# One pass of a GLA + S5 + RG-LRU trunk layer: six bands of GLA moved into the LRU stage, with changes of order in S5, merge and tail

## The reference

```
mod  = silu(c) @ w_ada + b_ada                   # shift, scale, gate, twice
proj = (x * (1 + scale1) + shift1) @ w_in        # q, k, v, r, glr, u, lx, ly, gates
LRU  : conv of lx, gates ga/gi (sigmoid), h_t = a_t h_(t-1) + sqrt(1-a_t^2) i_t x_t, both ways, * gelu(ly)
GLA  : log_a = log_sigmoid(glr @ w + b) / 16; chunked S_t = diag(a_t) S_(t-1) + k_t v_t, o_t = q_t S_t,
       both ways, normed, * silu(r)
S5   : h_t = A h_(t-1) + B u_t (complex), y = Re(C h) + d u, both ways; gelu; y * sigmoid(y @ w_glu)
merged = g_gla*(y_gla @ w) + g_s5*(y_s5 @ w) + g_lru*(y_lru @ w)     # g = sigmoid(gates)
x = layer_norm(alpha x + gate1 * (merged @ w_out))
y = layer_norm(alpha x + gate2 * (relu(mlp_in(x))^2 @ w_mlp_out))    # also returned: the final states
```

## Time and profile before

| what | us |
|---|---|
| runs | 3119.44, 3128.88, 3127.63 (median 3127.63) |
| the profiled execution, own time | 3128.83 |
| its span, first to last instruction | 3127.0 |
| TensorE (PE) busy | 2897.6 (93%) |
| VectorE (DVE) busy | 1786.0 (57%) |
| ScalarE (ACT) busy | 1163.8 (37%) |
| GpSimd (POOL) busy | 767.6 (25%) |
| mean granted TensorE clock | 0.963 of full |

### The profile page before, as it was taken

The page is one execution under the profiler, slowest core; times in us unless marked ns, Lnnn a source line. Parts: engine busy times, 40 slices in busy tenths (PEclk is TensorE's granted clock), DMA queues, the critical chain, the costliest instruction groups (busy, mean ns, idle before and its releaser), DMA issues. The chain is left out here.

```text
span 3127.0 us, 41861 instructions
## 1 busy us (share of the span) xinstructions
PE 2897.6 (93%) x17008; PEld 2795.7 (89%) x17008; DVE 1786.0 (57%) x2397; ACT 1163.8 (37%) x1761; POOL 767.6 (25%) x363
## 2 busy tenths in 40 slices
...
PEclk9999988989999699899998999999999999999998
...
GB/s 215 52 64 60 64 19 63 31 26 29 42 32 21 54 98 171 123 118 126 130 98 166 112 191 122 205 132 164 84 34 41 48 41 41 42 47 41 41 44 65
DMA packets 111164, 257.82 MB, mean 82 GB/s; under 512 B 20944, under 2 KB 54736, under 8 KB 110736
## 3 DMA queue, kind: packets, MB, share of 16 engines
...
...
## 5 line engine op out<-in xcount | busy, mean ns | idle before, releaser
L2539 PE MATMUL bank<-yhi,mrg_hi 128*128 128x384 f32 x1560 | 526.3, 337 | 3.3 <-POOL mrg_lo L2482 1.8
L2539 PE MATMUL bank<-ylo,mrg_hi 128*128 128x384 f32 x1560 | 522.9, 335 | 0.0
L2539 PE MATMUL bank<-yhi,mrg_lo 128*128 128x384 f32 x1560 | 522.8, 335 | 0.0
L2482 POOL TENSOR_TENSOR mrg_lo<-mrg_raw,mrg_hi 128x1024 fp32r<-128x1024 f32 x69 | 169.5, 2457 | 678.5 <-ACT mrg_hi L2641 678.5
L2506 PE MATMUL bank<-yhi,mrg_hi 128*128 128x384 f32 x864 | 293.0, 339 | 39.9 <-POOL mrg_lo L167 24.3
L2539 PEld LDWEIGHTS bank<-yhi,mrg_hi 128*128 128x128 f32 x1560 | 293.9, 188 | 6.9 <-POOL mrg_lo L2482 2.6
L2539 PEld LDWEIGHTS bank<-ylo,mrg_hi 128*128 128x128 f32 x1560 | 293.8, 188 | 1.2 <-issue 0.3
L2539 PEld LDWEIGHTS bank<-yhi,mrg_lo 128*128 128x128 f32 x1560 | 293.8, 188 | 0.0
L2506 PE MATMUL bank<-ylo,mrg_hi 128*128 128x384 f32 x864 | 290.8, 337 | 0.0
L2506 PE MATMUL bank<-yhi,mrg_lo 128*128 128x384 f32 x864 | 290.7, 336 | 0.0
L1720 PE MATMUL bank<-hhi,s_hi 128*128 128x384 f32 x768 | 265.1, 345 | 22.5 <-POOL s_lo L180 19.3
...
## 6 DMA issues: line engine op xcount, KB each, us to landing
...
```

Of the source, the lines that this page charges most:

```text
L2482: pool.tensor_tensor(WLO[SLOT[u]], S.raw[u % 2], WHI[SLOT[u]].bitcast(F32), ALU.subtract).then_inc(S.split_done, 1)
L2539: mm = pe.matmul(out, wt[SLOT[u]][:, w], r[:, k, band_cols(b)], start=(k == first and y == 0), stop=(k == last and y == 2))
```

## The change

- The weight buffers belong to `Core` and are shared by all stages. The LRU stage loads four of GLA's units, splits three, and TensorE makes six GLA bands behind the last LRU gate products, into banks 0, 1, 5, 6, 7, 2. ACT's `evac_y(11)` stands behind `roots(11)`. GLA begins with the evacuation of six bands, then band 6.
- S5: the tables' stores move up in SP's queue, between u loads; two lead bands stand behind `transposes(0)`; `powers` is cut in two and moved behind bands 6, 7, 9 and 10; four bands a slot for ten slots (was eleven), two in the last (was one).
- Merge: fills 4 to 8 on ACT and 4 to 7 on DVE are made inside the last GLU round; the load of a later tile is issued by another rule; the second tile of LRU weights is loaded ahead of the `y_out` wait.
- Tail: running sums on POOL, `rstd` of the last band ahead of six of eight `final`, sum of squares in halves, the last two `final` on DVE, y stored in other pieces.

The diff without context (line numbers of the old file; indentation inside a hunk reduced; "..." marks hunks that only pass names):

```diff
@@ L56
+AHEAD = 2
+AHEAD_BANK = (0, 1, 5, 6, 7, 2)
@@ L105
+self.raw, self.hi, self.lo = ([ctx.enter_context(nc.sbuf_tensor(f"w_{part}{s}", [P, UW], dt)) for s in range(2)]
+                              for part, dt in (("raw", F32), ("hi", F32R), ("lo", F32R)))
@@ L126
-def __init__(self, core, ctx, name, raw_width=UW):
-    nc = core.nc
+def __init__(self, core, name):
-    self.memory = ctx.enter_context(nc.sbuf_tensor(f"{name}_raw", [P, 2 * raw_width], F32))
-    self.raw = [self.memory[:, s * raw_width:s * raw_width + UW] for s in range(2)]
-    self.hi = [ctx.enter_context(nc.sbuf_tensor(f"{name}_hi{s}", [P, UW], F32R)) for s in range(2)]
-    self.lo = [ctx.enter_context(nc.sbuf_tensor(f"{name}_lo{s}", [P, UW], F32R)) for s in range(2)]
+    self.raw, self.hi, self.lo = [r[:] for r in core.raw], core.hi, core.lo
...
@@ L268
+gla_mm = sem("gla_mm")
+NEXT = 2 * LBLK
@@ L276
+def source(u):
+    return dram["lru_units"][u] if u < NEXT else dram["gla_units"][u - NEXT]
 def load_x(i):
-    if i < LBLK:
-        S.load(sync, 2 * i, 0, dram["lru_units"][2 * i])
+    if i < LBLK + 2:
+        S.load(sync, 2 * i, 0, source(2 * i))
 def load_y(i):
-    if i < LBLK:
-        S.load(sync, 2 * i + 1, 1, dram["lru_units"][2 * i + 1])
+    if i < LBLK + 2:
+        S.load(sync, 2 * i + 1, 1, source(2 * i + 1))
@@ L350
+sync.wait_ge(S.raw_in[1], 16 * (LBLK + 2))
+sync.wait_ge(S.split_done, 2 + NEXT + 3)
+sync.wait_ge(gla_mm, AHEAD * NB)
@@ L364
-if i + 1 < LBLK:
-    S.split_lo(pool, 2 * i + 3, 1)
-if i + 2 < LBLK:
-    S.split_lo(pool, 2 * i + 4, 0)
+S.split_lo(pool, 2 * i + 3, 1)
+S.split_lo(pool, 2 * i + 4, 0)
@@ L432
+pe.wait_ge(x_free, NB * LBLK)
+pe.wait_ge(g_free, GN * LBLK)
+for n in range(AHEAD * NB):
+    if n == AHEAD * NB - 1:
+        pe.wait_ge(y_free, NB * LBLK)
+    band(NEXT + n // NB, n % NB, core.bank[AHEAD_BANK[n]][:, 0:BW]).then_inc(gla_mm, 1)
 def unit_hi(u):
-    if u < 2 * LBLK:
-        if u >= 2:
+    if u == NEXT + 2:
+        act.wait_ge(gla_mm, NB)
+    if u <= NEXT + 2:
+        if 2 <= u < NEXT + 2:
@@ L542
-    if b == 1 and i:
+    if b == 1 and 0 < i < LBLK - 1:
-unit_hi(2 * i + 4)
+if i + 1 < LBLK:
+    unit_hi(2 * i + 4)
@@ L555
+evac_y(LBLK - 1)
+unit_hi(NEXT + 2)
...
@@ L859
+def band_bank(n):
+    return core.bank[AHEAD_BANK[n] if n < AHEAD * NB else n % 2][:, 0:BW]
     def _(sync):
-        sync.sem_inc(S.split_done, 2)
+        sync.sem_inc(S.split_done, 2 + AHEAD + 1)
+        sync.sem_inc(S.hi_done, AHEAD + 1)
+        for par in range(2):
+            sync.sem_inc(S.raw_in[par], 32)
+        sync.sem_inc(band_mm, AHEAD * NB)
@@ L883
-load(0)
-load(1)
-for u in range(2, 7):
+for u in range(4, 7):
@@ L928
-for u in range(len(UNITS)):
+for u in range(AHEAD + 1, len(UNITS)):
@@ L937
-if n >= 2:
-    pe.wait_ge(band_free, n - 1)
-out = core.bank[n % 2][:, 0:BW]
+pe.wait_ge(band_free, n - 1 if n >= AHEAD * NB + 2 else n - AHEAD * NB + 1)
+out = band_bank(n)
@@ L1023
-for n in range(NB):
-    band(n)
-pe.wait_ge(band_free, NB)
+band(AHEAD * NB)
+pe.wait_ge(band_free, AHEAD * NB)
-for n in range(NB, 4 * NB):
+for n in range(AHEAD * NB + 1, 4 * NB):
@@ L1055
 def unit_hi(u):
-    if u < len(UNITS):
-        if u >= 2:
-            act.wait_ge(band_mm, NB * (u - 1))
+    if AHEAD < u < len(UNITS):
+        act.wait_ge(band_mm, NB * (u - 1))
-    src = core.bank[n % 2][:, 0:BW]
+    src = band_bank(n)
@@ L1146
-unit_hi(0)
-unit_hi(1)
+for n in range(AHEAD * NB):
+    evac_band(n)
-for n in range(NB):
-    evac_band(n)
-for n in range(NB, 3 * NB):
+for n in range(AHEAD * NB, 3 * NB):
@@ L1429
+HELD = 2
-S = Stream(core, ctx, "s5")
+S = Stream(core, "s5")
@@ L1514
 def bands(n, slot):
-    per = [4 if k < 11 else 3 for k in range(LAST)] + [0]
+    per = [4 if k < 10 else 3 for k in range(LAST)] + [0]
@@ L1573
-for m in range(2, UNITS_U):
-    S.load(sync, m, m % 2, dram["s5_units"][m])
-    store_u(m - 2)
-for m in (UNITS_U, UNITS_U + 1):
-    S.load(sync, m, m % 2, dram["s5_units"][m])
-    store_u(m - 2)
@@ L1587
-for q in range(4):
-    store_tab(q)
-    if q == 0:
-        sync.wait_ge(lag_done, 1)
-        sync.dma_start(dram["kd"].rearrange("(b g) j d i -> (g j) b d i", g=P // S5I)[:, :, SCH - 1, :],
-                       lag0[:]).then_inc(lag_out, 16)
-    if q < 3:
-        u = UNITS_U + 2 + q
-        S.load(sync, u, u % 2, dram["s5_units"][u])
+def load_unit(u):
+    S.load(sync, u, u % 2, dram["s5_units"][u])
+for m in range(2, UNITS_U - 1):
+    load_unit(m)
+    store_u(m - 2)
+load_unit(UNITS_U - 1)
+store_tab(0)
+sync.wait_ge(lag_done, 1)
+sync.dma_start(dram["kd"].rearrange("(b g) j d i -> (g j) b d i", g=P // S5I)[:, :, SCH - 1, :],
+               lag0[:]).then_inc(lag_out, 16)
+store_u(UNITS_U - 3)
+load_unit(UNITS_U)
+store_u(UNITS_U - 2)
+load_unit(UNITS_U + 1)
+store_tab(1)
+load_unit(UNITS_U + 2)
+store_u(UNITS_U - 1)
+load_unit(UNITS_U + 3)
+store_tab(2)
+load_unit(UNITS_U + 4)
+store_tab(3)
+load_unit(UNITS_U + 5)
@@ L1608
-for b in range(BANDS_U, BANDS_U + LEAD):
-    if b % NB == 0 and b // NB + 2 >= UNITS_U + 5:
-        u = b // NB + 2
-        S.load(sync, u, u % 2, dram["s5_units"][u])
-        S.load(sync, u, u % 2, dram["s5_units"][u])
+        load_unit(u)
@@ L1792
-for b in range(BANDS_U // 2, BANDS_U + LEAD):
+for b in range(BANDS_U // 2, BANDS_U + LEAD - HELD):
+for b in range(BANDS_U + LEAD - HELD, BANDS_U + LEAD):
+    band(b)
@@ L1833
-def powers(c):
+def input_powers(c):
+def output_powers(c):
@@ L1927
-for b in range(3):
+for b in range(BANDS_U):
-act.wait_ge(pw_done, 1)
-act.wait_ge(p_in, 16 * 11)
-for c in range(2):
-    powers(c)
-for b in range(3, BANDS_U):
-    evac_u(b)
-for b in range(BANDS_U, BANDS_U + LEAD):
+    if b == 6:
+        act.wait_ge(pw_done, 1)
+        act.wait_ge(p_in, 16 * 11)
+    if b in (6, 7):
+        input_powers(b - 6)
+    if b in (9, 10):
+        output_powers(b - 9)
+for b in range(BANDS_U, BANDS_U + LEAD - HELD):
+evac_t(0)
-evac_t(0)
+for b in range(BANDS_U + LEAD - HELD, BANDS_U + LEAD):
+    evac_gate(b)
...
@@ L2240
+def deviation(q):
+    return mt[0] if q == 2 * NB - 1 else sd
...
@@ L2305
+TAIL = len(VISITS) - NB * KD
@@ L2346
-if n:
+if 1 <= n < 4:
+elif n >= 6:
+    act.wait_ge(filled, f - 1)
+    issue(act, n + 2)
@@ L2395
+lru_units(1)
-lru_units(1)
@@ L2446
+def store_y(b, k0, k1):
+    sync.dma_start(dram["y"].rearrange("k p t -> p k t")[:, k0:k1, band_cols(b)],
+                   x1[:, k0:k1, band_cols(b)]).then_inc(y_stored, 16)
-    for half in range(2):
-        ks = slice(half * KD // 2, (half + 1) * KD // 2)
-        sync.wait_ge(out_done, KD * b + KD // 2 * (half + 1))
-        sync.dma_start(dram["y"].rearrange("k p t -> p k t")[:, ks, band_cols(b)],
-                       x1[:, ks, band_cols(b)]).then_inc(y_stored, 16)
-sync.wait_ge(y_stored, 32 * NB)
+    sync.wait_ge(out_done, KD * b + KD // 2)
+    store_y(b, 0, KD // 2)
+    if b < NB - 1:
+        sync.wait_ge(out_done, KD * b + KD)
+        store_y(b, KD // 2, KD)
+sync.wait_ge(out_done, KD * NB - 2)
+store_y(NB - 1, KD // 2, KD - 2)
+sync.wait_ge(last_done, 2)
+store_y(NB - 1, KD - 2, KD)
+sync.wait_ge(y_stored, 32 * NB + 16)
@@ L2481
+for n in range(TAIL, len(VISITS)):
+    kind, i, m, b, u = VISITS[n]
+    if m == KD - 1:
+        continue
+    xs, xk = xsum[:, band_cols(b)], x1[:, m, band_cols(b)]
+    pool.wait_ge(dve_free, FREED[n][1])
+    if m == 1:
+        ins = pool.tensor_tensor(xs, x1[:, 0, band_cols(b)], xk, ALU.add)
+    elif m:
+        pool.wait_ge(tail_sum, (KD - 2) * b + m - 1)
+        ins = pool.tensor_tensor(xs, xs, xk, ALU.add)
+    if m:
+        ins.then_inc(tail_sum, 1)
@@ L2624
+    if m == 4:
+        act.wait_ge(filled, KD + 4)
+        issue(act, 7)
+    if m == KD - 1:
+        for n in range(4, 9):
+            fill_act(act, n)
-for n in range(4, 12):
+for n in range(9, 12):
@@ L2681
-if q:
+dev = deviation(q)
+if 0 < q < 2 * NB - 1:
-act.activation(sd, core.bank[7][:, 0:BW], ACT.Ln, bias=eps[:, 0:1]).then_inc(sd_s, 1)
+act.activation(dev, core.bank[7][:, 0:BW], ACT.Ln, bias=eps[:, 0:1]).then_inc(sd_s, 1)
-act.activation(sd, sd, ACT.Exp, scale=-0.5).then_inc(rs_done, 1)
+act.activation(dev, dev, ACT.Exp, scale=-0.5).then_inc(rs_done, 1)
@@ L2764
-for k in range(KD):
+for k in range(2):
-for k in range(KD):
+for k in range(2, KD):
+    final(1, k)
+for k in range(KD - 2):
@@ L2778
+if m == KD - 1:
+    for n in range(4, 8):
+        fill_dve(dve, n)
@@ L2786
-for n in range(4, 12):
+for n in range(8, 12):
@@ L2903
+def spread_halves(q):
+    dve.wait_ge(var_mm, q)
+    for half in range(2):
+        dve.wait_ge(sq_done, 2 * q + half + 1)
+        s4 = sq[:, half * KD // 2:(half + 1) * KD // 2]
+        st(dve.tensor_tensor(s4[:, 0:2], s4[:, 0:2], s4[:, 2:4], ALU.add))
+        if half == 0:
+            st(dve.tensor_tensor(s4[:, 0], s4[:, 0], s4[:, 1], ALU.add))
+    st(dve.tensor_tensor(s4[:, 0], s4[:, 0], s4[:, 1], ALU.add))
+    dve.tensor_tensor(qs, sq[:, 0], sq[:, KD // 2], ALU.add).then_inc(qs_done, 1)
```

(24 more changed lines are left out.)

4 lines of the change are left out of this document (2 added, 2 removed).

## The result

The changed kernel took 3087.24 us (median of 4 runs, 3082.61 to 3091.03), the one before 3126.16 (4 runs). The ratio is 0.9878, 95% interval 0.9856 to 0.9900: faster by 39 us or 1.2%, where 3045 and a gain of 83 were forecast. The time lies 17 us above the range. The profiled execution of the changed kernel took 3088.82 us.

A forecast was written before the change was run, and what follows sets the result against it. TensorE (PE), busy 93% of the 3127.0 us span, was taken as the bound, so time could come only from its holes. 33.7 + 26.1 + 19.4 + 3.9 = 83.1 off 3128.8 gave 3045 us; range 3026 to 3070.

The forecast's parts named there:

- part A: GLA's first six bands run inside the LRU stage: keys' transposes at 505.5 against 539.17, -33.7 us.
- PE now sets the end: LRU stage's end: TensorE ends the six bands at 473.1, DVE's last work done by then; new stage at 474.2.
- Part B: S5's opening: waits of TensorE and DVE go, -26.1 us, bounds -21.5 and -29.
- the four holes: S5's opening: DVE's 24.73 us before table 2, TensorE's 9.54 and 13.31, and 3.2 of `powers` all go.
- The 4.6 us for `input_weights(1)`: S5: TensorE may stand up to 4.6 us at the second transposes, most of it only a shift.
- Part C: Merge: fills made ahead, seven steps at 1.56 instead of 3.09 us; -19.4 us, bounds -10 and -20.5.
- Part D: Tail: running sums on POOL, `final` reordered around the last Ln; -3.9 us, bounds -5 and +4.6.
- Rival 2: S5 and merge: 4.6 us at `transposes(1)` stays, merge steps run at 2.33, not 1.56 (5.3 us); 3055, chance 0.18.
- Rival 3: Tail: POOL's adds hold up DVE, so the tail gives +0.6 instead of -3.9 us; 3049.5, chance 0.08.
- Rival 1: S5's opening: `tabq` not free early, DVE's 24.7 us stay on the path; 3067, chance 0.12.
- Rival 4: Slower than before: chip holds TensorE at 1.2 GHz some 185 us longer; 3137, chance 0.02.
- Rival 5: LRU stage: a semaphore keeps the ahead bands out of the hole, losing some 15 us; 3060, chance 0.05.

The follow-up runs named there:

- e4: The kernel before with only the six weight buffers allocated once, ahead of `mod`, and shared by all stages; no instruction moves: 3159.30 us.
- e1: The changed kernel with the 384-byte buffer `mod` allocated ahead of the shared weight buffers instead of behind them: 3061.59 us.
- e5: e1 with two waits on GpSimd, so the splits of GLA's units 1 and 2 wait for DVE's last LRU scan and multiply: 3063.58 us.
- e8: e1 with the tail's running sums on DVE again instead of GpSimd: 3065.53 us.
- e6: e1 with GpSimd's `input_weights(1)` ahead of the split of unit 13 instead of behind it: 3048.72 us.
- e7: e1 with four bands in eleven slots of S5's loop and one in the last, as before the change: 3063.69 us.
- e9: The changed kernel with the edits of e1, e5, e6 and e7 together: 3048.62 us.

## Why the prediction was wrong

**The step that failed** is the last sentence of part A: "Shared buffers alone cost and give nothing: addresses change, no instruction." The addresses cost 35.2 us in the kernel before (e4) and 25.6 in the changed one (e1). I had looked at what each edit does to instructions, waits and queues. In merge the stage was 18.3 us late, and 15.6 of it were this alone (e1: 1423.3 us, forecast 1420.6). A 384-byte buffer behind the weights instead of ahead of them decided. Of the miss of 42.2 us (3087.24 against 3045) 25.6 are this step's. The profile of e1 is late against the forecast by 4.9 us in LRU, 10.2 in S5 and 2.7 in merge, and ahead by 3.8 in GLA, where it has no dip of the clock.

**Part A** without the cadence: the first keys came at 513.7 us in e1, not 505.5. Of the 8.2 us, 4.9 lie in the LRU stage (479.1 for 474.2): "PE now sets the end" was wrong, DVE still does: the next stage starts 4.1 to 4.2 us behind its last multiply in the kernel before, in e1 and in e5 alike, whether TensorE ends its bands ahead of that multiply (e5) or behind it (e1). The two new splits on GpSimd hold two of its scans by 2.1 us each, of which e5 brings 2.4 back; another 1.6 were there ahead of the scans in e1 and not in e5. The other 3.3 lie in GLA's opening, which ran partly at the lower clock (0.76 over 480 to 500 us in e1). The wait of 3.0 us on ACT's evacuation came (2.8 in the changed kernel, 1.3 in e1). The first of the six new bands began at 448.85 in e1 (445.2 in e5), for the forecast's 445.0, behind 3.07 us of idle; the clock was 0.66 over 448 to 453 us and 1.00 behind, so the six bands took 26.7 us and not the 28.1 that the sum gave them. The first of them took 5.6 to 5.8 us where TensorE had stood still for 3.1 us before it (changed, e1, e8), and 4.2 to 4.3 behind 1.0 to 2.2 us (e5, e6, e7, e9). The gap of 3.1 us in front of the first moved band is just above the sign (under 3), and the seventh band has one of 4.1 us (4.5 in e1) of its own.

**Part B**: the four holes went. DVE's first `states` begins 28.3 us earlier in its stage in e1, against 26.1 forecast. The 4.6 us for `input_weights(1)` was right in kind (6.46), and I took it for a mere shift. What I missed is that the same GpSimd work, moved beside DVE's first item, slows DVE, which at 23.94 busy of 25.00 us has nothing to give: the first item grew from 25.5 to 30.9 us, and from the first item's start to the last one's are 378.9 us for 365.0. And the slots, costed at nothing, cost between nothing and 3.9. So -15.9 in e1 for -26.1.

**Part C** was nearly right: at the end of the branch products, of which it speaks, merge had gained 16.5 us in e1 for the 19.4 forecast, and 19.5 up to the last mean, with 0.5 of it from D. The steps run without waits but two of 1.5 and 1.6 us. The `ylo` total, where under 3 was the sign, is 5.7 in e1: these two (3.1), four short waits at the start of the stage's first product (1.8), which the kernel before has as well, and one later on (0.7). **Part D** was half as large as said: -1.1 from the last mean on and -0.5 ahead of it.

**The rivals.** Rival 2 had the place of the S5 loss and half of its size. Rival 3 had the right mechanism, and put it in the tail, where it costs under 1 us; it acts in the LRU stage's end and in S5's loop. (Its row has one stretched add; the trace has a second, of 1.86 us, and both lie beside a split of GpSimd.) Rivals 1, 4 and 5 did not come. None spoke of a matmul that becomes slower at the full clock.

One reading at the prediction's head is too strong, though no term hangs on it: the chain of waits is not nearly all TensorE, but TensorE to 36% of the span out of the 47% that it names.
